# Square sums of q and k as two fp32r matmuls, and the first branch weights split in the last chunk

## The reference, cut to what matters

```python
def l2norm(a):
    return a * lax.rsqrt(jnp.sum(a * a, axis=-1, keepdims=True) + EPS)

proj = jnp.einsum('bld,de->ble', h, w_in)
qkv, conv_buf_new = short_conv(gdn_qkv, conv_buf, gdn_conv)      # 4 taps, then silu
q = l2norm(to_heads(cq, GDN_HEADS)) * (GDN_DK ** -0.5)
k = l2norm(to_heads(ck, GDN_HEADS))
o, s_gdn_new = gdn_recurrence(q, k, v, g, beta, s_gdn)           # chunks of tokens
y_gdn = (head_rmsnorm(o, gdn_norm) * silu(gdn_z)) @ gdn_wo       # gla_wo, pool_wo likewise
merged = g0 * y_gla + g1 * y_pool + g2 * y_gdn                   # sigmoid gates
y = merged @ w_out
x = x + rmsnorm(y, norm_post)
```

## Time and profile before

| | us |
|---|---|
| median of 3 runs | 2467.62 |
| lowest and highest | 2466.26, 2468.43 |
| the profiled execution's own time | 2469.36 |
| its span, first to last instruction | 2467.6 |
| TensorE busy | 2403.4 (97%) |
| GpSimd busy | 897.3 (36%) |

### The profile page before, as it was taken

The page is one execution under the profiler, slowest core; times in us unless marked ns, Lnnn a source line. Parts: engine busy times, 40 slices in busy tenths (PEclk is TensorE's granted clock), DMA queues, the critical chain, the costliest instruction groups (busy, mean ns, idle before and its releaser), DMA issues. The chain is left out here.

```text
span 2467.6 us, 37963 instructions
## 1 busy us (share of the span) xinstructions
PE 2403.4 (97%) x14719; PEld 2246.3 (91%) x14719; DVE 1191.9 (48%) x1955; ACT 714.0 (29%) x1439; POOL 897.3 (36%) x792
## 2 busy tenths in 40 slices
PE   7999999999999999999999999999999989999997
PEld 6989999999999999997999999899999989999786
DVE  5720111222466665005666666566666553325886
ACT  6311111111145441113233322333323242223433
POOL 1212112111112112215555665556655433334554
PEclk9999999999999999999999999999999999999999
DMA  5213422100111122141432234632343075554443
GB/s 169 76 70 113 193 78 78 44 35 35 70 45 60 52 91 86 56 139 51 132 91 86 80 107 127 221 86 80 94 122 100 33 265 210 191 174 145 136 160 116
DMA packets 192579, 265.00 MB, mean 107 GB/s; under 512 B 15072, under 2 KB 167920, under 8 KB 186992
## 3 DMA queue, kind: packets, MB, share of 16 engines
q1 hardware_dynamic: 192496, 263.86, 33.0%
HBM read 164.54 MB, written 99.29 MB: 107 GB/s over the span
## 5 line engine op out<-in xcount | busy, mean ns | idle before, releaser
L393 PE MATMUL dense<-h,w_hi 128*128 128x416 f32 (+1 forms) x1640 | 590.6, 360 | 0.0
L394 PE MATMUL dense<-h,w_hi 128*128 128x416 f32 (+1 forms) x1640 | 582.5, 355 | 0.0
L395 PE MATMUL dense<-h,w_lo 128*128 128x416 f32 (+1 forms) x1640 | 581.8, 355 | 0.0
L188 POOL TENSOR_TENSOR w_hi<-w_raw,zero 128x1024 fp32r<-128x1024 f32 x77 | 149.0, 1935 | 1091.5 <-PE dense L395 795.4
L1444 PE MATMUL gate_bank<-h,w_hi 128*128 128x352 f32 x1632 | 422.3, 340 | 0.0
L393 PEld LDWEIGHTS dense<-h,w_hi 128*128 128x128 f32 x1640 | 310.3, 189 | 13.4 <-issue 6.2
L394 PEld LDWEIGHTS dense<-h,w_hi 128*128 128x128 f32 x1640 | 308.9, 188 | 11.3 <-issue 4.5
L395 PEld LDWEIGHTS dense<-h,w_lo 128*128 128x128 f32 x1640 | 309.3, 189 | 7.1
L1444 PEld LDWEIGHTS gate_bank<-h,w_hi 128*128 128x128 f32 x1632 | 272.7, 189 | 8.8 <-issue 0.7
L1444 PE MATMUL gate_bank<-h,w_lo 128*128 128x352 f32 x816 | 263.7, 323 | 0.0
L2593 PE MATMUL y<-o_hi,wo_hi 128*128 128x352 f32 x576 | 187.9, 326 | 7.3 <-PEq L107 6.6
(11 more groups left out here) (266 smaller groups left out, 4104.1 us busy)
## 6 DMA issues: line engine op xcount, KB each, us to landing
w_raw<-in_w_in SPq DMA_DIRECT2D x77, 512.0 KB, 5.9
rows_then_inputs<-scratch_feat SPq DMA_DIRECT2D x16, 1856.0 KB, 9.4
scratch_feat<-row_y SPq DMA_DIRECT2D x28, 1056.0 KB, 4.9
gate<-scratch_gates SPq DMA_DIRECT2D x11, 2112.0 KB, 8.7
scratch_gates<-gate_row SPq DMA_DIRECT2D x102, 176.0 KB, 1.8
o_raw<-scratch_branch_out SPq DMA_DIRECT2D x6, 2112.0 KB, 13.1
scratch_h_second<-h SPq DMA_DIRECT2D x2, 4224.0 KB, 19.4
h<-scratch_h_second SPq DMA_DIRECT2D x6, 1408.0 KB, 7.7
```

The costliest lines, as they stand in the source:

```text
L188: nc.gpsimd.tensor_tensor(self.hi[:, p], raw, zeros, ALU.add).then_inc(self.high_ready, 1)
L393: nc.tensor.matmul(out, w_hi[:, p, k], hi.tile(k, t), start=(k == 0), stop=False)
L394: nc.tensor.matmul(out, w_hi[:, p, k], lo.tile(k, t), start=False, stop=False)
L395: mm = nc.tensor.matmul(out, w_lo[:, p, k], hi.tile(k, t), start=False, stop=(k == KD - 1))
```

## The change

Three parts go together.

First, the square sums. After the squares, ScalarE also copies each tile of T into an fp32r tile `sq_hi` of two slots (`square_high`): tiles 0 and 1 behind the squares, tiles 2 and 3 behind the first two logarithms, tile 4 behind the next two. GpSimd subtracts it from T in place, into `sq_lo`, an fp32r view of T (`square_low`). TensorE then runs two fp32r matmuls a tile with an fp32r copy of the ones, high and low part into the same bank, and waits per tile for the subtraction (`sq_split`).

Second, GpSimd's program. In slots 0 to 9 its loop over weight blocks is written out: a slot's tiles 2 to 4 are subtracted ahead of the split of the next block's weights, the following block's tiles 0 and 1 behind it.

Third, the last chunk. SP issues the early loads when the last gate product is done, ahead of its last gate store. ScalarE rounds the first branch weights behind its copy of U, ahead of both head norms, and VectorE takes their difference ahead of its scaling of the outputs; both leave the tail.

```diff
+        sq_hi = rounded_at("sq_hi", first.bytes_at + 4 * rows[2], SQ_SLOTS * SIG_W)
+        sq_lo = rounded_at("sq_lo", first.bytes_at + 4 * rows[1], NT)
+        ones_r = rounded_at("ones_r", first.bytes_at + 4 * rows[3], P)
...
+                def square_low(j, t):
+                    pool.wait_ge(sq_high, j * PROJ_TILES + t + 1)
+                    nc.gpsimd.tensor_tensor(sq_lo[:, span(t)], T[:, span(t)],
+                                            sq_hi[:, t % SQ_SLOTS, 0:width(t)].bitcast(F32), ALU.subtract).then_inc(sq_split, 1)
+                split_blocks(2, (F_CONV + 1) // 2)
+                for j in range(10):
+                    f = F_CONV + 1 + j
+                    if j >= 2:
+                        for t in range(SQ_SLOTS, PROJ_TILES):
+                            square_low(j - 2, t)
+                    pool.wait_ge(dense_ready, (f - 1) * PROJ_TILES)
+                    weights.split(nc, pool, f // 2, f, f % 2)
+                    if 1 <= j <= 8:
+                        for t in range(SQ_SLOTS):
+                            square_low(j - 1, t)
+                split_blocks((F_CONV + 11) // 2, F_LATE // 2)
...
-                        if tile == 0:
-                            pe.wait_ge(squares_ready, j + 1)
...
-                            nc.tensor.matmul(side[:, (t + odd) % 2, 0:width(t)], ones, T[:, span(t)],
-                                             start=True, stop=True).then_inc(side_ready, 1)
+                            pe.wait_ge(sq_split, j * PROJ_TILES + t + 1)
+                            nc.tensor.matmul(side[:, (t + odd) % 2, 0:width(t)], ones_r[:, :],
+                                             sq_hi[:, t % SQ_SLOTS, 0:width(t)], start=True, stop=False)
+                            nc.tensor.matmul(side[:, (t + odd) % 2, 0:width(t)], ones_r[:, :], sq_lo[:, span(t)],
+                                             start=False, stop=True).then_inc(side_ready, 1)
...
+                def square_high(j, t):
+                    act.wait_ge(squares_ready, j + 1)
+                    last = max(u for u in range(PROJ_TILES) if u % SQ_SLOTS == t % SQ_SLOTS)
+                    before = (j - 1) * PROJ_TILES + last if t < SQ_SLOTS else j * PROJ_TILES + (t - SQ_SLOTS)
+                    if not isinstance(j, int) or before >= 0:
+                        act.wait_ge(side_ready, before + 6 * PROJ_TILES + 1)
+                    nc.scalar.copy(sq_hi[:, t % SQ_SLOTS, 0:width(t)],
+                                   T[:, span(t)]).then_inc(sq_high, 1)
...
                             for u in range(2 * t, min(2 * t + 2, PROJ_TILES)):
                                 norm_logs(j - 2, u, 1 - p)
+                            for u in range(2 * t + 2, min(2 * t + 4, PROJ_TILES)):
+                                square_high(j - 2, u)
...
                         if t == 3 and square:
                             squares(j - 1, 1 - p)
+                            for u in range(SQ_SLOTS):
+                                square_high(j - 1, u)
...
+                nc.scalar.copy(ones_r[:, :], ones)
...
+                        if then is not None and T == TILES - 1:
+                            then()
                         sp.wait_ge(gate_taken, c * TILES + (T + 3))
...
-                gate_traffic(CHUNKS, 1, None)
-                sp.wait_ge(out_stored, 16 * 5)
-                sp.wait_ge(outg_stored, 16 * 5)
-                for q in range(2):
-                    sp.wait_ge(gate_stored[q], 16 * ((CHUNKS // 2 + 1) * TILES // 2 + 1))
-                late.load_in_chunk_phase(sp, d)
+                def load_late():
+                    sp.wait_ge(gate_ready, (CHUNKS + 1) * TILES)
+                    sp.wait_ge(out_stored, 16 * 5)
+                    sp.wait_ge(outg_stored, 16 * 5)
+                    late.load_in_chunk_phase(sp, d)
+                gate_traffic(CHUNKS, 1, None, then=load_late)
...
                     copy(U[0:n], ring[2][0:n]).then_inc(S["U_taken"], 1)
+                    if then is None:
+                        early_split.high_weights(act, nc, late)
                     before(act, "outg_ready", c)
...
+                    if then is None:
+                        early_split.low_weights(dve, nc, late)
                     scale_outputs("Og", 1, "rsg_ready")
```

More of the change, by code:

```diff
@@ L137, in __init__ @@
         words = 2 * self.ROWS * P + 2 * HEADS * P
+        self.bytes_at = (nc.sbuf_base + 31) // 32 * 32
         self.bytes = context.enter_context(nc.sbuf_tensor("rows_then_inputs", [P, words], F32))
@@ L281, in project_phase, with rounded_at @@
         pool_w = first.at(rows[3], rows[4]).rearrange("p (g m) -> p g m", g=4)
+        SQ_SLOTS = 2
+        assert rows[3] + P <= rows[4]
+        def rounded_at(name, offset, words):
+            pad = offset % 32 // 4
+            tile = nc.alloc_sbuf_tensor_at(name, [P, pad + words], F32R, offset=offset - 4 * pad)
+            return tile[:, pad:pad + words]
+        sq_hi = rounded_at("sq_hi", first.bytes_at + 4 * rows[2], SQ_SLOTS * SIG_W) \
+            .rearrange("p (s t) -> p s t", s=SQ_SLOTS)
+        sq_lo = rounded_at("sq_lo", first.bytes_at + 4 * rows[1], NT)
+        ones_r = rounded_at("ones_r", first.bytes_at + 4 * rows[3], P)
         Y = sb("row_y", [P, 2, ROW])
@@ L346, in project_phase @@
         squares_ready = sem("squares_ready")
+        sq_high, sq_split = sem("sq_high"), sem("sq_split")
         norm_ready = sem("norm_ready")
@@ L367, in _, with split_blocks @@
                     weights.split(nc, pool, 1, 2 + p, p)
-                with pool.Fori(2, F_LATE // 2) as i:
-                    for p in range(2):
-                        pool.wait_ge(dense_ready, i * (2 * PROJ_TILES) + (p - 1) * PROJ_TILES)
-                        weights.split(nc, pool, i, i * 2 + p, p)
+                def split_blocks(first_pair, last_pair):
+                    with pool.Fori(first_pair, last_pair) as i:
+                        for p in range(2):
+                            pool.wait_ge(dense_ready, i * (2 * PROJ_TILES) + (p - 1) * PROJ_TILES)
+                            weights.split(nc, pool, i, i * 2 + p, p)
+                def square_low(j, t):
[14 more added lines that the diff above has]
+                split_blocks((F_CONV + 11) // 2, F_LATE // 2)
                 pool.wait_ge(dense_ready, (F_LATE - 2) * PROJ_TILES)
@@ L1302, in good, with gate_traffic @@
                     sp.sem_inc(h_good[t], CHUNKS // 2)
-                def gate_traffic(c, half, next_half, swap=False):
+                def gate_traffic(c, half, next_half, swap=False, then=None):
                     if next_half is not None:
@@ L2143, in __init__, with high_weights @@
         self.o_high, self.o_split = (held.add(nc.alloc_semaphore(n)) for n in ("o_high", "o_split"))
+    def high_weights(self, act, nc, late):
+        act.wait_ge(late.wo_landed[0], 16)
+        nc.scalar.copy(self.wo_hi[:, :, :], late.wo_ring[:, 0]).then_inc(self.wo_high, 1)
     def high(self, act, nc, late):
@@ L2147, in high, with low_weights @@
         nc.scalar.copy(self.o_hi[0][:, :, :], late.o_raw[:, 0:4]).then_inc(self.o_high, 1)
-        act.wait_ge(late.wo_landed[0], 16)
-        nc.scalar.copy(self.wo_hi[:, :, :], late.wo_ring[:, 0]).then_inc(self.wo_high, 1)
         nc.scalar.copy(self.o_hi[1][:, :, :], late.o_raw[:, 4:8]).then_inc(self.o_high, 1)
+    def low_weights(self, dve, nc, late):
+        dve.wait_ge(self.wo_high, 1)
+        nc.vector.tensor_tensor(self.wo_lo[:, :, :], late.wo_ring[:, 0], self.wo_hi[:, :, :].bitcast(F32),
+                                ALU.subtract).then_inc(self.wo_split, 1)
     def low(self, dve, nc, late):
-        def difference(lo, raw, hi):
-            return nc.vector.tensor_tensor(lo[:, :, :], raw, hi[:, :, :].bitcast(F32), ALU.subtract)
         dve.wait_ge(self.o_high, 1)
-        difference(self.o_lo[0], late.o_raw[:, 0:4], self.o_hi[0]).then_inc(self.o_split, 1)
-        dve.wait_ge(self.wo_high, 1)
-        difference(self.wo_lo, late.wo_ring[:, 0], self.wo_hi).then_inc(self.wo_split, 1)
+        nc.vector.tensor_tensor(self.o_lo[0][:, :, :], late.o_raw[:, 0:4], self.o_hi[0][:, :, :].bitcast(F32),
+                                ALU.subtract).then_inc(self.o_split, 1)
 PRODUCTS = 7
```

## The result

The changed kernel takes 2472.35 us in the median of 20 runs, the kernel before 2469.45 in the median of 20 (the three runs shown ahead of the prediction had 2467.62). The ratio is 1.0014, with a 95% interval from 1.0008 to 1.0020: slower by 2.9 us between the medians, and within the 0.2% that I had called no change. I had forecast 2482.3 us, 12.9 to 14.7 above before, and had given no change a chance of 0.12.

What follows compares the result with a forecast made beforehand. TensorE, busy for 97% of the span, was taken to bound the kernel. 2469.36 + 15.4 for the convolution blocks - 0.7 for the chunk phase's end = 2484.1, 2482.3 us as a median; range 2471 to 2497.

Steps and rivals of the forecast that it cites:

- The matmuls: TensorE's square sums: fp32r pairs in place of fp32 sums free 1.63 us a block, 13.0 us in eight blocks.
- The copies: ScalarE's rounding copy of each tile of squares takes 0.53 us for 416 columns.
- The subtraction: GpSimd's subtraction for each tile takes 1.09 us at 416 columns, with bounds of 0.98 and 1.29.
- My own lower bound: GpSimd's subtraction at 0.98 us in place of 1.09, which makes the blocks' sum +11 us.
- The turns at the port: Convolution blocks: GpSimd and VectorE's two-input products block each other at SBUF for whole instructions; blocks of 28.68 us, +15.4 in all.
- The squares' end: Repeating block: normalising product ends 0.6 us behind ScalarE's table load, so squares end with TensorE's tile 4 at 28.68.
- The order at the first long product: VectorE's first long product holds the port from 4.64 to 6.91, ahead of GpSimd's subtraction of tile 2.
- The end of the chunk phase: Last chunk: early weight loads and split leave the tail; -0.7 us, between a gain of 1.2 and a loss of 0.5.
- The free port: Rival: convolution products don't hold GpSimd up, only the block's start waits; 26.7 us a block, 2467.4 in all; chance 0.12.
- The lows hidden: Rival: subtractions end before TensorE wants them, so the whole 13.0 + 0.7 us comes, 2453.9; chance 0.05.
- The clock in the blocks: Rival: TensorE's idling at each block's start drops it to 1.2 GHz, 13.6 us more, 2495.9; chance 0.08 for most blocks.
- The fourth rival: Two fp32r matmuls take 0.70 us again, so the 13.0 us saved is gone and waits stay, 2495.3; chance 0.05.

Runs made afterwards that it cites:

- vector_tile4: Changed kernel with subtractions on VectorE, weight split later, squares in two parts, tile 4's subtraction behind the first long product: 2454.79 us, ratio 0.9930 to 0.9957.
- dearer_lows: Changed kernel with five one-element memsets on GpSimd ahead of every subtraction: blocks of 27.37 us, 2476.94 us in one run.
- split_behind: Changed kernel with the weight split's high part waiting for the convolution's end, its low part for the normalising product: blocks 27.08 us, 2473.49 us (one run).
- vector_first_12: Changed kernel with twelve one-element memsets on GpSimd ahead of tile 2's subtraction: blocks of 27.30 to 27.39 us, 2472.25 us (one run).
- no_lows: Changed kernel without GpSimd's subtractions, second matmul rereading the rounded squares: blocks 25.07 us, 2468.31 us (one run); run again 2457.02 us.
- vector_first: Changed kernel with three one-element memsets on GpSimd ahead of tile 2's subtraction: blocks of 27.19 us, 2473.12 us (one run).

## Why the prediction was wrong, by its own steps

**The matmuls** were right: 1.63 us a block forecast, and `vector_tile4`, in which TensorE waits for no pair, is 1.68 below the kernel before.

**The copies** were right: 0.53 forecast, 0.54 measured.

**The subtraction** was mis-sized: 1.09 forecast, 0.92 measured (0.99 for 448 columns), below the lower bound of 0.98 that I had given. Both are 2.2 ns a column, with no fixed part that shows. My line was drawn through the 352-column row, whose 0.94 us is nearly as much as 448 columns take here. `dearer_lows` prices this step: with each subtraction 0.17 later the block is 27.37 in place of 27.09. So the price, together with the turned order at the port that this run also has, accounts for 0.28 of the 1.59 us a block by which I was too high; the growth lies in the two waits ahead of that turn. My own lower bound, +11 in all, was still far above +3.24.

**The turns at the port** were right as a mechanism and wrong in their sum, and this is the step that failed. With the price and the order that I had assumed, `dearer_lows` measures 27.37 where I had 28.68. TensorE's waits, forecast against that run: ahead of tile 0's pair 1.77 against 1.19, tile 1's 0.70 against 0.57, tile 2's 0.37 against none, tile 3's 0.94 against 0.43; the low matmuls that follow late, 0.30 a block in all, stood in no term. These differences make up 1.29 of the 1.31. Set from TensorE's end of tile 4, forecast against the same run: tile 2's subtraction ends at 8.06 against 6.96, tile 3's at 9.43 against 8.02, tile 4's at 12.79 against 10.97, the split's high part at 14.96 against 12.82, its low part at 19.63 against 17.23, the normalising product at 22.27 against 19.58. Of these last 2.69 us, 0.6 is there from the squares on; the other 2.1 grew at one turn after another. I had charged each with a semaphore and the whole duration. The rows show less, and I read them so that the waiting instruction has begun already and has only the rest to do: tile 2's subtraction ends 0.84 after the product (753.30 to 754.14) and not 1.15, and a long product ends 2.15 after GpSimd (756.97 to 759.12 in the changed kernel) and not 2.35. The short products, for which I had put 0.28, cost nothing that shows: tile 3's subtraction starts 0.13 behind tile 2's, with five memsets between, and takes its own 0.93.

**The squares' end** at zero followed from that sum. I had the normalising product 0.6 behind the table load; it was 0.38 ahead (0.8 in `dearer_lows`). A chain that would have closed on itself for 0.62 us a block in seven blocks hung on a margin of 0.6, and the turns ahead of it were overpriced by 2.1. So of the 1.59 us a block the turns and the squares' end that followed from them make 1.31, which is most of what lies between +15.4 and +3.24; and `split_behind` shows that nothing of the split reaches the squares.

**The order at the first long product** went the other way, GpSimd first by 0.06 us. `vector_first_12` prices it at 0.2 to 0.3. In my sum both were ready at the same hundredth, 4.64, and I didn't say that this was a choice.

**The end of the chunk phase** was right in place and near in size: -0.7 forecast, -0.87 in two traces. Its parts, in the order of SP, ScalarE and TensorE of the kernel after:

```profile
1982.33 0.34 SPq L2152 DMA_DIRECT2D wo_ring<-in_wo  x1
...
1998.48 0.53 SPq L1386 DMA_DIRECT2D scratch_branch_out<-out_gdn  x1
...
1993.15 1.37 ACT L2209 CAST o_hi<-o_raw 128x1408 fp32r<-128x1408 f32 x1 [0.28 <-DMA o_raw<-scratch_branch_out]
...
2001.04 0.63 PE L2655 MATMUL y<-o_hi,wo_hi 128*128 128x352 f32 x1 [5.71 <-PEq L107]
```

The branch outputs are there 0.28 us after ScalarE is ready for them, where the earlier trace rows show 2.37, and SP's last store issue is next late, as I had said. The closing phase then took 469.2 us in place of 468.4; a half-clock stretch reached 5.2 us into it in place of 4.5, which by half its length explains about 0.4 of the 0.8. The rest I did not trace, but it need not belong to the change: over the fifteen traces the closing phase takes 468.1 to 469.8 us with the same code, and one kernel run twice (`no_lows`, `no_lows_again`) has 468.7 and 469.8.

**The rivals.** The free port was wrong as a mechanism though its time, 2467.4, was nearer than mine. The lows hidden didn't happen in this kernel; `vector_tile4` shows what it is worth, 2454.8 where I had 2453.9. The clock in the blocks stayed at 1.00 in the changed kernel, over three waits a block. The fourth rival did not happen either: the pairs take 0.38 and 0.41.

## What to carry to other kernels

Work that moves between an engine with slack and the bound is judged by its latency at the place where the bound waits: five subtractions of 0.92 us cost 2.02 us a block because they sat behind the squares and in turn with another engine's products, and the same five at 0.59 us, put between that engine's own products and with the squares in two parts, made TensorE wait for nothing. When a schedule worked out closes a loop from one block into the next, write down the margin by which it closes; if that is smaller than the number of steps times what each may be off, give both cases as forecasts of their own. Compare kernels by the stage that was changed before comparing whole times.

## What the runs showed of the hardware

**The clock at the hand-over.** Where the projection ends and the chunk phase starts, TensorE stands still for 3.2 to 3.3 us (before and `no_lows`). In the traces of before and after no half-clock stretch follows; in the other thirteen one of 3.4 or 6.8 us does, within 20 us, and in one of them (`no_lows`) another of 23.9, behind a second stop of 1.6 us; `vector_first` has such a second stop too, and no fall behind it. The same kernel as `no_lows` run again had 3.4. So executions of one kernel can differ by 12 us, half of 23.9, at a place that no edit touched.

**The order at the port.** A subtraction whose row starts 0.04 us after a product's was served ahead of it, and one 0.33 after was not. An instruction that waits for its turn shows its start when it began to wait, and its end comes 0.1 to 0.2 us sooner after the other's end than its own duration says (0.84 for 0.99, 2.15 for 2.35).
